# Three passes of rounded parts for the latent tiles of the even stage's output product

## The chip, the cores and the metric

The kernel runs on one core of a Trainium2 chip. A core has TensorE (PE, matrix products into PSUM banks of 128x512 fp32), VectorE (DVE), ScalarE (ACT), GpSimd (POOL) and SyncE (SP), which issues most of the DMAs. The metric is the device time of one execution in microseconds; lower is better.

## The reference

Two blocks of layers work on 256 tokens of 1024 features, in fp32: a windowed attention layer, an expert layer, a recurrent layer and a second expert layer, then an "even" and an "odd" mixing layer. The change lies in the even mixer. It adds the outputs of two attention forms, a gated linear attention (GLA, 4 heads of 128) and a latent attention (MLA, 8 heads of 64), side by side as 1024 features, and multiplies them by one output matrix:

```python
# latent attention of the even mixer, 8 heads, keys = 256 context tokens + 256 tokens
s = (einsum('bqhd,bkhd->bhqk', q_nope, k_nope) + einsum('bqhr,bkr->bhqk', q_rope, k_rope)) * MLA_SCALE
p = softmax(s, axis=-1)
y_m = einsum('bhqk,bkhd->bqhd', p, v).reshape(B, L, 512) * silu(mg)
# y_g: the gated linear attention's output, 512 features
y_lat = einsum('bne,ed->bnd', concatenate([y_g, y_m], -1), w_out)      # 1024 x 1024
x = layer_norm_2(ALPHA * x + gate * y_lat, g, b)
```

## The kernel before

Tokens are held as two halves of 128. Features across partitions are held as tiles of 128: `B.yT` has eight tiles j of 128 features by 256 tokens. Tiles 0 to 3 come from the GLA and 4 to 7 from the latent attention; `GH` is 4 and `T` is 8.

**Two kinds of products.** A product of plain fp32 tiles is one call of `matmul` (L371) and leaves two records in the trace. Where an operand is split into a rounded part (type fp32r, `hi`) and the rest (`lo = x - hi`), `product` (L367 to L374) makes three calls, lo by hi, hi by lo and hi by hi, with one record each. Most weight products of the even and odd stage are of the second kind. `split_weights_scalar` (L396) has ScalarE write the rounded part of a weight unit in four pieces of 128x1024, and `split_weights_vector` (L412) has VectorE write the rest over the raw unit. The even stage's output product is of the first kind, for all its eight tiles.

**The latent rounds.** The even stage interleaves two generators on each engine, a linear one (GLA) and a latent one, one step of each in turn (`even_order`, L2218). After projections come the latent rounds n = 0 to 19 of `latent_tensor`, `latent_vector` and `latent_scalar`; a unit of work i is one head and one half of the tokens, sixteen in all (`NB`). In round n each engine does, in this order:

- TensorE: the scores of n (L2761), four transposes of the probabilities of n-2 (L2773), and in rounds 6, 10, 14 and 18 the value products of latent tile j (L2786) into bank 7. Its linear step follows: GLA's turned output (L2551), then for half 0 and then half 1 one GLA tile of the output product per step, in both column blocks c of 512.
- VectorE: reciprocal and scaling of the probabilities of n-2 (L2843, L2845), then maximum and its negative of the scores of n (L2849, L2851), and in rounds 7, 11, 15 and 19 the gated y of latent tile j (L2861), which writes `B.yT[:, GH + j]`. Its linear steps at this time are the scaled GLA rows (L2638, after rounds 7 and 8) and GLA's gated y (L2648, after rounds 9 and 10).
- ScalarE: exp of the scores of n (L2907), then the copy of the transposed probabilities of n-2 (L2915). After round 14 it rounds pieces 0 and 1 of the odd stage's first weight unit (`odd_sv`), and VectorE subtracts them after round 17.

TensorE's transposes i wait for the event `probs_lat` i, and for the exp of i+1, which frees their bank. The engines work strictly in the order of the program.

**Behind the rounds.** TensorE does the latent tiles of the output product, for half 0 block 0, half 0 block 1, half 1 block 0 and half 1 block 1 (`even_tensor`, L2296 to L2303). After each of these four it tells `out_product`. VectorE then subtracts pieces 2 and 3 of `odd_sv`, and `gated_residual_vector` (L2192) multiplies each block by the gate (L2202), adds it to x (L2204), takes its moments (L514), and norms each half after its second block (L529, L533). The odd stage starts from the normed half 0 on ScalarE (`flat_scalar`, L2172 to L2183), whose rows TensorE transposes (L2088). In between TensorE does two modulation blocks (L964), whose weights SyncE loads into slots that are free after the last latent y.

**Memory.** `even_out0` and `even_out1` are units of the weight ring; each holds its eight tiles as 8 x 512 columns, tiles 4 to 7 in the second half.

Of the kernel before, what the change touches and what calls it, by code (L numbers as in the profile page):

```python
# [9 lines left out]
F32R = mybir.dt.float32r  # L10
ACT = mybir.ActivationFunctionType
ALU = mybir.AluOpType
AX = mybir.AxisListType

P = 128
D = 1024
S = 256
H = S // P
T = D // P
# [4 lines left out]
UNIT = 4096  # L24
# [25 lines left out]
GH, GK, GV, GR, GCH = 4, 64, 128, 16, 64  # L50
# [12 lines left out]
NB = MH * H  # L63
# [283 lines left out]
class Program:  # L347
# [1920 lines left out]
    def even_tensor(self):  # L2268
        sig, pe, B, K = self.sig, self.pe, self.B, self.B.bank
# [26 lines left out]
        _, banks, y, y_event, names, _ = self.even_out()  # L2296
        w = self.out_weights(names)
        for half in range(H):
            for c in range(2):
                for j in range(GH, T):  # L2300
                    pe.wait_ge(*sig.after(*y_event(j)))
                    last = self.out_step(banks[2 * half + c], y, w[c], j, half)
                last.then_inc(*sig.tell("out_product", ("out_product", "even", half, c), ("free", names[c])))  # L2303
# [125 lines left out]


# [360 lines left out]
    def latent_vector(self):  # L2791
        sig, v, B, K = self.sig, self.v, self.B, self.B.bank
# [37 lines left out]
        for j in range(MH // 2):  # L2830
            n = 2 * j
# [7 lines left out]
        for n in range(NB + 4):  # L2839
            if 2 <= n < NB + 2:  # L2840
                i = n - 2
# [15 lines left out]
            if n >= 7 and n % 4 == 3:  # L2857
                j = n // 4 - 1
                v.wait_ge(*sig.after("values_lat", j))
                v.wait_ge(*sig.after("even_taken", "mg0" if j < 2 else "mg2"))  # L2860
                v.tensor_tensor(B.yT[:, GH + j, :], K[7][:, j % 2 * S:(j % 2 + 1) * S], B.mgT[:, j, :], ALU.mult).then_inc(  # L2861
                    *sig.tell("mla_y", ("mla_y", j), ("free", "latents")))
            if n == NB + 1:
                self.split_weights_vector("odd_sv", pieces=(0, 1))
            yield

    def latent_scalar(self):
        sig, a, B, K = self.sig, self.a, self.B, self.B.bank
# [20 lines left out]
        for j in range(MH // 2):  # L2889
            n = 2 * j + 1  # L2890
# [7 lines left out]
        for n in range(NB + 4):  # L2898
# [10 lines left out]
            if 2 <= n < NB + 2:  # L2909
                i = n - 2  # L2910
                h, half = i // H, i % H
# [5 lines left out]
            if n == NB - 2:  # L2917
                self.split_weights_scalar("odd_sv", pieces=(0, 1))
# [325 lines left out]
def buffers(nc, ctx):  # L3244
# [116 lines left out]
    B.yT, B.mgT = M.take("even_yT", T, S), M.take("mgT", GH, S)  # L3361
# [12 lines left out]
    B.att = [M.place(f"att{dd}", h_at + 2048 + 1024 * dd, [4, 2 * P]) for dd in range(2)]  # L3374
    flat_at = M.at
# [11 lines left out]
    B.gla_ss, B.gla_r = M.take("gla_ss", H * GH), M.take("gla_r", H * GH)  # L3387
    M.at = ring + TAIL_SLOT * UNIT
# [62 lines left out]
```

## Time and profile before

| | |
|---|---|
| median of 3 runs | 1420.01 us (1419.85 to 1422.73) |
| profiled execution | 1421.49 us |
| its span | 1419.6 us |
| TensorE busy | 1101.4 us, 78% |
| VectorE busy | 467.2 us, 33% |
| ScalarE busy | 321.2 us, 23% |
| mean granted TensorE clock | 0.893 |

The span is the time from the first to the last instruction of the profiled execution. Most of it, up to about 1140 us, is the experts' weights coming in; the even stage takes the stretch from there to about 1316 us, the odd stage the rest. In rows, "PE" is a matrix product and "PEld" the load of its stationary operand; "xN" is a count of merged instructions, and the time beside it is from the start of the first to the end of the last. A name such as L2845 is a line of the kernel.

### The profile page before, as it was taken

The page shows a single profiled execution, that of the slowest core. Times are in us where ns is not written, and L with a number is a line of the kernel's source. Part 1 is how long each engine was busy: PE and PEld are TensorE (multiplying, and loading weights), DVE is VectorE, ACT ScalarE, POOL GpSimd, SP SyncE. Part 2 cuts the span into 40 slices and gives each one's busy share as a digit, 9 for nine tenths or more (in the row PEclk, how much of TensorE's full clock was granted, in tenths as well). Part 3 has the DMA queues.
Part 4 walks back from the last instruction along what each step waited for, and adds up shares of the span by engine and source line. Part 5 has one row for each costly group of instructions (what it writes and reads, how often), then busy time and mean ns, then how long its engine had stood idle before and what let it go on. Part 6 is the DMA issues. An engine that isn't in the chain of part 4 may idle for free.

```text
span 1419.6 us, 19300 instructions
## 1 busy us (share of the span) xinstructions
PE 1101.4 (78%) x8457; PEld 624.6 (44%) x8457; DVE 467.2 (33%) x952; ACT 321.2 (23%) x618; POOL 86.2 (6%) x114
## 2 busy tenths in 40 slices
PE   8999756598486556999995656766655699999998
PEld 7657312263131112897641211111111279754997
DVE  6636203101110000777630100100000077666774
ACT  4502110000410000465220000000000046543640
POOL 1311100000000000040120000000000000000100
PEclk9999978899688878999997777767898899999999
DMA  9977999999999999958999999999999974113720
GB/s 372 425 292 298 423 427 428 427 428 425 428 427 427 427 427 422 388 201 343 427 383 426 428 427 427 428 427 428 428 427 428 422 308 156 60 74 157 301 95 30
DMA packets 43211, 501.27 MB, mean 353 GB/s; under 512 B 6654, under 2 KB 8148, under 8 KB 13688
## 3 DMA queue, kind: packets, MB, share of 16 engines
q1 hardware_dynamic: 38432, 491.91, 82.9%
q10 hardware_dynamic: 2696, 6.83, 1.3%
q8 instruction: 67, 1.10, 0.3%
q0 software_dynamic: 2000, 1.29, 0.3%
q14 instruction: 16, 0.13, 0.0%
HBM read 498.92 MB, written 1.10 MB: 352 GB/s over the span
## 4 chain that ended last, share of the span: by engine, by line
DMA 45%; PE 42%; DVE 6%; ACT 4%; SPq 1%; issue 1%; POOL 0%; DVEq 0%; ACTq 0%; POOLq 0%
DMA weight_ring<-in_moe_w_gate_up 32%; DMA weight_ring<-in_u_down 8%; PE bank L1437 7%; PE bank L371 5%; PE bank L372 3%; PE bank L374 3%; PE bank L373 3%; PE bank L1467 3%; DMA weight_ring<-in_u_ctx_kv 2%; PE bank L1888 2%; PE bank L653 2%; DMA weight_ring<-in_u_last 2%; DVE weight_ring_rounded L412 2%; SPq L570 1%; PE bank L1079 1%
## 5 line engine op out<-in xcount | busy, mean ns | idle before, releaser
L1437 PE MATMUL bank<-weight_ring,expert_tokens 128*32 128x512 f32 x1920 | 282.3, 722 | 156.5 <-DMA weight_ring<-in_moe_w_gate_up 151.6
L1437 PEld LDWEIGHTS bank<-weight_ring,expert_tokens 128*32 128x32 f32 x1920 | 61.4, 121 | 354.3 <-DMA weight_ring<-in_moe_w_gate_up 197.1
L1467 PE MATMUL bank<-weight_ring,actT 128*32 128x256 f32 x1760 | 141.1, 479 | 56.6 <-DMA weight_ring<-in_u_down 46.9
L1676 DVE TENSOR_TENSOR act<-silu,bank 128x256 f32<-128x256 f32 x32 | 13.5, 420 | 387.2 <-ACT silu L1794 387.2
L1467 PEld LDWEIGHTS bank<-weight_ring,actT 128*32 128x32 f32 x1760 | 65.1, 133 | 122.6 <-issue 48.4
L1794 ACT ACTIVATE silu<-bank 128x256 f32<-128x256 f32 x32 | 12.3, 384 | 436.7 <-PE bank L1437 436.6
L1690 DVE COPY expert_outs<-bank 32x256 f32<-32x256 f32 x60 | 25.1, 418 | 236.0 <-PE bank L1467 235.0
L412 DVE TENSOR_TENSOR weight_ring_rounded<-weight_ring,weight_ring_rounded 128x1024 fp32r<-128x1024 f32 (+1 forms) x76 | 89.3, 1234 | 11.4 <-ACT weight_ring_rounded L396 11.2
L396 ACT CAST weight_ring_rounded<-weight_ring 128x1024 fp32r<-128x1024 f32 (+1 forms) x72 | 69.9, 1045 | 19.1 <-DMA weight_ring<-in_u_even_narrow 8.2
L1811 ACT COPY expert_outs<-bank 32x256 f32<-32x256 f32 x60 | 21.9, 365 | 214.8 <-PE bank L1467 214.0
L539 POOL TENSOR_TENSOR norm_rstd<-norm_var,minus_half 128x1 f32<-128x1 f32 x12 | 11.2, 936 | 838.8 <-DVE norm_var L1725 642.2
L1449 PE MATMUL bank<-ident,act 128*128 128x128 f32 x64 | 17.1, 354 | 41.0 <-DVE act L1676 41.0
L1449 PEld LDWEIGHTS bank<-ident,act 128*128 128x128 f32 x64 | 10.1, 206 | 73.5 <-DVE act L1676 73.5
L417 PE MATMUL bank<-ident 128*128 128x128 f32 x278 | 36.9, 288 | 3.5 <-DMA ident<-in_k_ident 2.6
L417 PEld LDWEIGHTS bank<-ident 128*128 128x128 f32 x278 | 34.5, 201 | 5.7 <-DMA ident<-in_k_ident 2.6
L372 PE MATMUL bank<-odd_h_hi_rounded,weight_ring_rounded 128*128 128x256 f32 x128 | 36.4, 284 | 0.0
L374 PE MATMUL bank<-odd_h_hi_rounded,weight_ring_rounded 128*128 128x256 f32 x128 | 36.2, 283 | 0.0
L373 PE MATMUL bank<-odd_h_rounded,weight_ring_rounded 128*128 128x256 f32 x128 | 36.2, 283 | 0.0
L372 PE MATMUL bank<-even_h_hi_rounded,weight_ring_rounded 128*128 128x256 f32 x96 | 28.6, 298 | 2.5 <-DVE weight_ring_rounded L412 2.4
L371 PE MATMUL bank<-weight_ring,even_yT 128*128 128x512 f32 x64 | 29.3, 597 | 0.0
L371 PE MATMUL bank<-weight_ring,attention_out 128*128 128x512 f32 x64 | 28.1, 594 | 0.0
L1888 PE MATMUL bank<-convolved,weight_ring 128*128 128x256 f32 x128 | 27.8, 379 | 0.0
(528 smaller groups left out, 1848.1 us busy)
## 6 DMA issues: line engine op xcount, KB each, us to landing
weight_ring<-in_moe_w_gate_up SPq DMA_DIRECT2D x120, 2048.0 KB, 36.5
weight_ring<-in_u_down SPq DMA_DIRECT2D x55, 2048.0 KB, 37.1
weight_ring<-in_u_ada SPq DMA_DIRECT2D x8, 2048.0 KB, 11.3
weight_spare<-in_moe_w_gate_up SPq DMA_DIRECT2D x6, 2048.0 KB, 40.7
weight_spare<-in_u_down SPq DMA_DIRECT2D x5, 2048.0 KB, 40.7
weight_ring<-in_u_last SPq DMA_DIRECT2D x16, 512.0 KB, 34.0
weight_ring<-in_u_lru SPq DMA_DIRECT2D x4, 2048.0 KB, 20.8
weight_spare<-in_u_ada SPq DMA_DIRECT2D x3, 2048.0 KB, 13.7
```

Of the source, the lines that this page charges most:

```text
L371: return self.pe.matmul(out, sh, mh, start=start, stop=stop)
L372: self.pe.matmul(out, sl, mh, start=start, stop=False)
L373: self.pe.matmul(out, sh, ml, start=False, stop=False)
L374: return self.pe.matmul(out, sh, mh, start=False, stop=stop)
L396: a.copy(hi[:, c], raw[:, c]).then_inc(*sig.tell("weights_rounded", ("rounded", name, i)))
L412: v.tensor_tensor(lo[:, c], raw[:, c], hi[:, c], ALU.subtract).then_inc(*sig.tell("weights_split", ("weights", name, i)))
L417: self.pe.matmul(bank[:, 0:P], self.B.ident, self.B.ident, start=True, stop=True)
L653: last = pe.matmul(out, *operands, start=(parts == self.HIGH and t == 0 and first), stop=(parts == self.WEIGHTS_REST and t == T - 1), skip ...
L1437: last = pe.matmul(up[CAP * j:CAP * (j + 1), :], self.expert_tokens(t, e), w[:, :, j, :], start=(t == 0), stop=(t == T - 1))
L1449: last = pe.transpose(K[2][:, s * P:(s + 1) * P], B.act[i][:, s::2], B.ident)
L1467: last = pe.matmul(K[3][CAP * q:CAP * (q + 1), 0:QC], B.actT[i][:, s, j * CAP:(j + 1) * CAP], w[:, jj, s, q, :], start=(j == 0 and s == 0) ...
L1888: last = pe.matmul(self.lru_bank(job)[:, ff * S:(ff + 1) * S], w[:, z * LB + n, at:at + P], B.xc[:, 2 * n + c], start=(c == 0), stop=(c == 1))
```

## The change

The four latent tiles of the output product become products of rounded parts. For that:

- in rounds 7, 11, 15 and 19 VectorE forms y twice from PSUM, once as fp32 into `B.yT` and once rounded into `B.y_mla_hi`, and writes their difference over the fp32 one (`B.y_mla_lo`). The event `mla_y` j and the freeing of the latents' memory move to the second of these instructions; a new event `mla_split` j follows the third;
- the second halves of `even_out0` and `even_out1` are split in four pieces of 128x1024: ScalarE rounds piece i in round 8, 10, 12 and 14, after its copy, and waits for the turned GLA output before it; VectorE subtracts it at the end of round 9, 11, 13 and 15. The order is block 0 first piece, block 1 first piece, block 0 second piece, block 1 second piece;
- the latent tiles of each of the four output blocks are three calls per tile, in the order of blocks as before, with waits on `mla_split` and `out_split`;
- ScalarE's rounding of pieces 0 and 1 of `odd_sv` moves from after round 14 to after round 16;
- the new tiles are placed in memory (`mla_y_hi`, `even_out_hi0`, `even_out_hi1`; the differences lie over the raw data).

```diff
--- before.py
+++ after.py
@@ -2293,14 +2293,15 @@
             last.then_inc(*sig.tell("projected", ("even", job), *free))
 
         self.even_order("tensor", run, None, self.linear_tensor(), self.latent_tensor())
-        _, banks, y, y_event, names, _ = self.even_out()
-        w = self.out_weights(names)
-        for half in range(H):
-            for c in range(2):
-                for j in range(GH, T):
-                    pe.wait_ge(*sig.after(*y_event(j)))
-                    last = self.out_step(banks[2 * half + c], y, w[c], j, half)
-                last.then_inc(*sig.tell("out_product", ("out_product", "even", half, c), ("free", names[c])))
+        _, banks, _, _, names, _ = self.even_out()
+        for half, c in ((0, 0), (0, 1), (1, 0), (1, 1)):
+            rows = slice(half * P, (half + 1) * P)
+            for j in range(T - GH):
+                pe.wait_ge(*sig.after("mla_split", j))
+                pe.wait_ge(*sig.after("out_split", c, j // 2))
+                last = self.product(banks[2 * half + c], (B.y_mla_hi[:, j, rows], B.y_mla_lo[:, j, rows]),
+                                    (B.out_hi[c][:, j, :], B.out_lo[c][:, j, :]), start=False, stop=(j == T - GH - 1))
+            last.then_inc(*sig.tell("out_product", ("out_product", "even", half, c), ("free", names[c])))
 
     def even_narrow_tensor(self, w, h):
 
@@ -2427,6 +2428,24 @@
         self.flat_pool("odd", 1)
 
 
+
+    OUT_PIECES = ((0, 0), (1, 0), (0, 1), (1, 1))
+
+    def out_weights_scalar(self, i):
+
+        sig, a, B = self.sig, self.a, self.B
+        c, q = self.OUT_PIECES[i]
+        flat = lambda w: w[c][:, 2 * q:2 * q + 2, :].rearrange("p t c -> p (t c)")
+        a.wait_ge(*sig.after("gla_turned", 1))
+        a.wait_ge(*sig.after("arrived", f"even_out{c}"))
+        a.copy(flat(B.out_hi), flat(B.out_raw)).then_inc(*sig.tell("out_rounded", ("out_rounded", c, q)))
+
+    def out_weights_vector(self, i):
+        sig, v, B = self.sig, self.v, self.B
+        c, q = self.OUT_PIECES[i]
+        flat = lambda w: w[c][:, 2 * q:2 * q + 2, :].rearrange("p t c -> p (t c)")
+        v.wait_ge(*sig.after("out_rounded", c, q))
+        v.tensor_tensor(flat(B.out_lo), flat(B.out_raw), flat(B.out_hi), ALU.subtract).then_inc(*sig.tell("out_split", ("out_split", c, q)))
 
     def odd_or_even(self, buf, kk):
 
@@ -2859,7 +2878,14 @@
                 v.wait_ge(*sig.after("values_lat", j))
                 v.wait_ge(*sig.after("even_taken", "mg0" if j < 2 else "mg2"))
                 v.tensor_tensor(B.yT[:, GH + j, :], K[7][:, j % 2 * S:(j % 2 + 1) * S], B.mgT[:, j, :], ALU.mult).then_inc(
+                    *sig.tell("mla_y", ("mla_y_whole", j)))
+                v.tensor_tensor(B.y_mla_hi[:, j, :], K[7][:, j % 2 * S:(j % 2 + 1) * S], B.mgT[:, j, :], ALU.mult).then_inc(
                     *sig.tell("mla_y", ("mla_y", j), ("free", "latents")))
+                v.wait_ge(*sig.after("mla_y", j))
+                v.tensor_tensor(B.y_mla_lo[:, j, :], B.yT[:, GH + j, :], B.y_mla_hi[:, j, :], ALU.subtract).then_inc(
+                    *sig.tell("mla_split", ("mla_split", j)))
+            if n in (9, 11, 13, 15):
+                self.out_weights_vector(n // 2 - 4)
             if n == NB + 1:
                 self.split_weights_vector("odd_sv", pieces=(0, 1))
             yield
@@ -2914,7 +2940,9 @@
                     a.wait_ge(*sig.after("values_lat", (h - 4) // 2))
                 a.copy(B.pT_lat[h % 4][:, :, half * P:(half + 1) * P], self.latent_bank("t", i).rearrange("p (a b) -> p a b", a=KT)).then_inc(
                     *sig.tell("scalar_moved", ("pT_lat", i)))
-            if n == NB - 2:
+            if n in (8, 10, 12, 14):
+                self.out_weights_scalar(n // 2 - 4)
+            if n == NB:
                 self.split_weights_scalar("odd_sv", pieces=(0, 1))
             yield
 
@@ -3358,7 +3386,8 @@
     B.lru_hi, B.lru_lo = M.take_both("lru_x_hi", T, S)[1], M.take_both("lru_x_lo", T, S)[1]
 
     M.at = room
-    B.yT, B.mgT = M.take("even_yT", T, S), M.take("mgT", GH, S)
+    (B.yT, low), B.mgT = M.take_both("even_yT", T, S), M.take("mgT", GH, S)
+    B.y_mla_lo = low[:, GH:T]
     B.reset, B.tri = M.take("reset", 2, S), M.take("tri", 2, P, dt=U32)
     at = M.at
     B.qT_gla, B.kT_gla = M.take("gla_qT", 2, S), M.take("gla_kT", 2, S)
@@ -3372,6 +3401,7 @@
     B.h_raw["even"], B.h_lo["even"] = M.take_both("even_h", T, S)
     B.state = [[M.place(f"state{dd}{i}", h_at + 256 * (2 * dd + i), [2, GV]) for i in range(2)] for dd in range(2)]
     B.att = [M.place(f"att{dd}", h_at + 2048 + 1024 * dd, [4, 2 * P]) for dd in range(2)]
+    B.y_mla_hi = M.place("mla_y_hi", h_at + 1024, [T - GH, S], F32R)
     flat_at = M.at
     B.flat_stats, B.flat_mv, B.flat_sum = M.take("flat_stats", 12), M.take("flat_mv", 2), M.take("flat_sum", 2)
     B.flat_rstd, B.flat_var, B.flat = M.take("flat_rstd", H), M.take("flat_var", H), M.take("flat", H, D)
@@ -3385,6 +3415,12 @@
     B.ke, B.qe, B.kend, B.qb = ([M.take(f"{n}{dd}", 2, S) for dd in range(2)] for n in ("ke", "qe", "kend", "qb"))
     B.o_gla, B.gla_junk = M.take("gla_out", H, GH * GV), M.place("gla_squares", flat_at, [H, GH * GV])
     B.gla_ss, B.gla_r = M.take("gla_ss", H * GH), M.take("gla_r", H * GH)
+    B.out_hi, B.out_raw, B.out_lo, B.one = [], [], [], M.place("one", M.size - UNIT - 8, [1])
+    for c in range(2):
+        slot = B.place_of[f"even_out{c}"]
+        B.out_hi.append(M.place(f"even_out_hi{c}", M.size - UNIT + c * UNIT // 2, [T - GH, 512], F32R))
+        for dst, ring_view in ((B.out_raw, B.slot), (B.out_lo, B.slot_r)):
+            dst.append(ring_view[slot][:, UNIT // 2:UNIT].rearrange("p (t c) -> p t c", t=T - GH))
     M.at = ring + TAIL_SLOT * UNIT
     B.cq, B.ckr = M.take("cq", H, QR), M.take("ckr", H, CKR)
     B.latT, B.krT = M.take("latT", KEYS), M.take("krT", KEYS)[0:MR, :]
```

## Rows read from the trace of the kernel before

**Rows 1.** Windows: us, busy PE, PEld, DVE, ACT, POOL, then clock, DMA share, GB/s
```profile
1262.00:1272.00 10.00, 7.33 (x43) 4.37 (x44) 8.32 (x23) 4.89 (x12) 1.00 (x1) 1.00 0.00 1
1272.00:1298.00 26.00, 26.00 (x111) 12.94 (x107) 10.74 (x27) 11.36 (x22) 0.00 (x0) 1.00 0.05 20
```

**Rows 2.** Chain of what ended last, even stage's end: start, us, what
```profile
1269.57 0.50 DVE mla_scores L2845
...
1298.01 7.08 PE bank L371 x16
...
1315.87 0.70 PE bank L2088 x4
```

**Rows 3.** Time line of TensorE: start, us, line, out<-in, [idle before <-releaser]
```profile
1264.95 0.63 PE L2773 MATMUL bank<-ident,mla_scores 128*128 128x128 f32 x4 [1.30 <-DVE mla_scores L2845]
...
1270.20 0.63 PE L2773 MATMUL bank<-ident,mla_scores 128*128 128x128 f32 x4 [1.14 <-DVE mla_scores L2845]
...
1278.33 0.60 PE L2773 MATMUL bank<-ident,mla_scores 128*128 128x128 f32 x4
...
1284.37 0.60 PE L2773 MATMUL bank<-ident,mla_scores 128*128 128x128 f32 x4
...
1291.63 0.63 PE L2773 MATMUL bank<-ident,mla_scores 128*128 128x128 f32 x4
...
1297.94 14.00 PE L371 MATMUL bank<-weight_ring,even_yT 128*128 128x512 f32 x32
```

**Rows 4.** Time line of VectorE, latent rounds, residual, and one later weight group
```profile
1276.31 0.41 DVE L2861 TENSOR_TENSOR even_yT<-bank,mgT 128x256 f32<-128x256 f32 x1
1276.64 0.15 DVE L2843 RECIPROCAL mla_tot<-mla_tot 128x1 f32<-128x1 f32 x1
1276.83 0.49 DVE L2845 TENSOR_SCALAR mla_scores<-mla_scores,mla_tot 128x512 f32<-128x512 f32 x1
...
1282.54 0.49 DVE L2845 TENSOR_SCALAR mla_scores<-mla_scores,mla_tot 128x512 f32<-128x512 f32 x1
...
1291.00 0.49 DVE L2845 TENSOR_SCALAR mla_scores<-mla_scores,mla_tot 128x512 f32<-128x512 f32 x1
...
1298.06 0.42 DVE L2861 TENSOR_TENSOR even_yT<-bank,mgT 128x256 f32<-128x256 f32 x1 [3.71 <-PE bank L2786]
1298.40 2.35 DVE L412 TENSOR_TENSOR weight_ring_rounded<-weight_ring,weight_ring_rounded 128x1024 fp32r<-128x1024 f32 x2
...
1305.11 0.69 DVE L2202 TENSOR_TENSOR even_tmp<-bank,gate 128x512 f32<-128x512 f32 x1 [1.22 <-PE bank L371]
...
1326.71 4.63 DVE L412 TENSOR_TENSOR weight_ring_rounded<-weight_ring,weight_ring_rounded 128x1024 fp32r<-128x1024 f32 x4 [0.24 <-ACT weight_ring_rounded L396]
```

**Rows 5.** Time line of TensorE, first and eighth record of the odd output product
```profile
1390.64 0.40 PE L372 MATMUL bank<-weight_ring_rounded,odd_yT_rounded 128*128 128x512 f32 x1
...
1392.25 0.39 PE L373 MATMUL bank<-weight_ring_rounded,odd_y_hi 128*128 128x512 f32 x1
```

**Rows 6.** Tile view of the modulation weights' loads (in_u_ada), issued at 1298.5 and 1298.9
```profile
DMA to landing us min/median/max: 7.5/10.4/13.3
```

**Rows 7.** Time line of ScalarE in the latent rounds
```profile
1266.30 0.58 ACT L2915 COPY mla_pT<-bank 128x512 f32<-128x512 f32 x1
...
1268.71 0.69 ACT L2907 ACTIVATE mla_scores<-bank,mla_neg 128x512 f32<-128x512 f32 x1 [1.83 <-DVE mla_neg L2851]
...
1286.63 2.00 ACT L396 CAST weight_ring_rounded<-weight_ring 128x1024 fp32r<-128x1024 f32 x2
...
1294.45 0.59 ACT L2915 COPY mla_pT<-bank 128x512 f32<-128x512 f32 x1 [1.57 <-PE bank L2773]
```

**Rows 8.** Waits from 1262 to 1298: who for whom, us in total, times, longest
```profile
DVE mla_neg L2849 <- PE bank L2761: 12.8, 7, 3.6
```

**Rows 9.** Window and TensorE's time line at the start of the even stage
```profile
1154.00:1162.00 8.00, 5.77 (x32) 5.32 (x30) 4.37 (x9) 6.58 (x14) 0.55 (x1) 0.79 1.00 428
...
1156.61 1.91 PE L2088 MATMUL bank<-ident,flat 128*128 128x128 f32 x8 [2.23 <-ACT flat L2164]
```

## The prediction

> **What bounds the kernel now.** I read the views from the coarse to the fine. First the windows of the latent rounds: TensorE is busy 26.00 of 26 us between 1272 and 1298, and 7.33 of 10 us between 1262 and 1272, where VectorE is busy 8.32 us [rows 1]. So there are two regimes: one stretch in which VectorE sets the pace, then one in which TensorE does. Then the chain of what ended last: at 1298.01 it runs through sixteen records of the output product, then through VectorE's residual and norm and ScalarE's flat rows, and at 1315.87 back to TensorE [rows 2]. Hence two questions. What does the added VectorE work do to the rounds, and how much of the shorter product reaches VectorE's residual?
>
> The third view is the time line of TensorE [rows 3]. I call the transposes of round i's probabilities t(i); they have L2773, and each stands behind VectorE's scaling of the probabilities at L2845, p(i). t(6) at 1264.95 and t(8) at 1270.20 wait for p (1.30 and 1.14 us idle). t(10), t(12) and t(14), at 1278.33, 1284.37 and 1291.63, show no idle time, but that alone says nothing on how much slack they have. For that the fourth view, VectorE's time line [rows 4]: p(10) begins at 1276.83 and takes 0.49, p(12) begins at 1282.54, p(14) at 1291.00. From the end of p(8), 1269.57 + 0.50 in the chain [rows 2], to t(8) there are about 0.15 us, so TensorE could have gone on at 1277.47, 1283.18 and 1291.64. The slack is 0.86 for t(10), 1.19 for t(12) and nothing for t(14): TensorE and VectorE arrive there together, though no view reports a wait.
>
> **The change, part by part.**
>
> *a. Three passes for four latent tiles.* Sixteen fp32 products (4 tiles, 2 halves, 2 column blocks), 32 records in 14.00 us from 1297.94, so a pace of 14.00 / 32 = 0.4375 with the overhang of the last record, 0.43 without, and 0.86 a product [rows 3]. The new products have 3 records of 128x512 of rounded parts. Their pace is that of the odd stage's output product: seven paces from 1390.64 to 1392.25, 0.230 each [rows 5]. The stationary part is reloaded before each there too, as it will be here. 48 records are 11.0 us instead of 13.8, and TensorE is done 2.8 us sooner. The path asks for another thing, the end of half 0, block 1, which is what VectorE waits for at 1305.11 [rows 4]. Before it lie 16 records, 6.88 us; then 24, 5.52 us: 1.36 sooner, at 1303.75. Is VectorE free for it by then? The first block comes after 12 x 0.23 = 2.8 us instead of 3.4, but VectorE has the steps of c and two weight pieces ahead of it, to 1298.06 + 1.13 + 2.35 = 1301.5. The first block's three steps, each of about 0.7 like that at 1305.11, end at 1303.6. So the second block's end rules, and this part is **minus 1.3** (minus 1.36, less what little VectorE may be late).
> What is late next: the modulation blocks at L964 follow the products. The second block of their weights lands 13.3 us after its issue, the largest of the two [rows 6], so near 1312.2, and the issue waits for the last y (about 0.4 us later now). 64 of 128 small products after that, 1.8 us, end at 1314.5; the half-0 transposes come at 1315.87 - 1.3 = 1314.6. Just covered; at worst 0.1 us. All of the odd stage's path behind it moves as one.
>
> *b. Weight pieces.* ScalarE rounds four pieces of 128x1024 and VectorE subtracts, in rounds 8, 10, 12, 14 and 9, 11, 13, 15. The weights themselves landed long before (output products use them from 1272 on without waiting). Price on VectorE: two such pieces take 2.35 us and four 4.63, so 1.14 each [rows 4]. Price on ScalarE: 1.0, two having taken 2.00; its copy of round 8 runs from 1266.30 to 1266.88, and the next exp is at 1268.71 [rows 7]. The new cast waits for the second group of turned gla tiles, which TensorE finishes where that copy ends; it fits before the exp. Behind the waiting cast are queued that exp and, on VectorE, the piece of round 9. So **ScalarE's part costs nothing**, with some 0.5 us of room in round 8 and more later; without that cover up to 1.0 us. Queued behind a VectorE piece are p(i) and, behind that, TensorE's t(i).
>
> *c. Rounded y.* The product y is formed twice from PSUM, then a subtraction waits for both. y to the next start is 0.33 [rows 4]; the second y adds 0.33, ends 0.42 after its start, the subtraction starts 0.04 later and holds the next for 0.34 (same 256 columns). From the first y's start to the next instruction: 0.33 + 0.42 + 0.04 + 0.34 = 1.13 instead of 0.34, **0.79 more** each, in rounds 7, 11, 15, 19. Bounds: 0.67 if the subtraction needs no wait, 0.9 if all three run their full 0.42 with a wait behind each. The row is exact for the product and near for the subtraction, so the middle.
> The Trainium skill, page "VectorE: DVE Perf Modes", section "The DRAIN you can't avoid", has the next instruction start only when the pipe is empty, and a semaphore costing nothing extra. The rows have y to the next start at 0.33 and its length at 0.42 [rows 4], so this trace doesn't agree for instructions that don't depend on one another. By the page c would be 0.93 and a piece 1.22, and the sum some 0.6 us more.
>
> *d. Where b and c meet the rounds.*
> Round 7: 0.79 lies before the scaled gla rows (L2638) and p(6), and t(6) already waits: **+0.79**. Everything up to t(8) moves along: VectorE's one gap in between waits for scores that TensorE, itself held by the gla rows, delivers later too.
> Round 9: 1.14 before gla's y and p(8), t(8) already waits: **+1.14**.
> Round 11: c and b, 1.93, before p(10), slack 0.86: **+1.07**.
> Round 13: b, 1.14, before p(12), slack 1.19: **0** (at most 0.1).
> Round 15: c and b, 1.93, before p(14), slack 0: **+1.93**.
> Between these, TensorE has 26.00 of 26 us and nothing is given back [rows 1]. Sum **+4.9**.
> Round 19: y(3) at 1298.06, its parts done 1.2 us later; tile 3 of the first block is reached 9 x 0.23 = 2.07 us after 1297.94. Hidden by 0.7 us.
>
> *e. Moved pieces of the odd weights.* ScalarE's two casts go from after round 14 to after round 16's copy: about 1292.9 to 1294.9, then the last copy of probabilities, old start 1294.45 [rows 7], comes some 0.4 late and ends at 1295.4, before the value products, which end at 1297.94. VectorE's two subtractions then end near 1296.2, before y(3) at 1298.06. Zero; if the cover went, 0.4.
>
> **Sum**: 0.79 + 1.14 + 1.07 + 1.93 - 1.3 = +3.6 us. The profiled execution is 1421.49 us with a span of 1419.6, and its sum is 1425.1. The median of the runs shown is 1420.01, 1.5 us below it; the same 3.6 on the median gives **1423.6**.
>
> **Rivals.**
> R1, cover: VectorE waits 12.8 us in all for TensorE's scores from 1262 to 1298 [rows 8], and the 6.9 us added there (3 x 0.79 + 4 x 1.14) would fit into that if they fell into the right places. Then the tail's -1.3 alone is left: 1418.7, not slower. Against it: both t(6) and t(8) wait on VectorE by name, and p(14) leaves no slack; idle time ahead of the scores is of no use to a step that stands behind them. It decides if p could be formed ahead of the new pieces, which the order in the file forbids.
> R2, half cover: only the two places where TensorE waits today grow (1.93), and rounds 11 and 15 hide theirs: 1.93 - 1.3 = +0.6, 1420.6. For it: no view shows a wait there. Against it: the worked slack.
> R3, the clock: TensorE stood still for 2.23 us before 1156.61, and over the 8 us from 1154 its granted clock averages 0.79, so it was at 1.2 GHz for part of them [rows 9]. The pauses at t(6), t(8) and t(14) grow to 2.09, 2.28 and 1.93. If one of them drops the clock, it costs what that stretch lost, 0.21 x 8 = 1.7 us: 1425.3; two, 1427. Against it: the pauses of 1.30 and 1.14 left it at 1.00 [rows 1]. [...]
> R4, no cheaper passes: were each of the three as long as a third of an fp32 product (0.285), a would bring nothing and the sum is +4.9, 1424.9. The odd stage's records speak against it.
>
> **Chances.** Forecast (+2.9 to +4.5) 0.56; R3 0.07; another added delay 0.05; R4 0.02; R2 and its neighbours 0.14; R1 0.12; something that I don't see and that gains 0.04. By these the low end is taken to 1420.2, so that R2 is in and R1 out, the high end to 1427.0 for R3; the unknown costs (0.36 for c, 0.6 for the drain, 0.4 for e) lie within. A measurement of this kernel can tell about 0.2%, 2.8 us, from no change. R1 and R2 lie within it. Even with every edit hidden, the path gains no more than 1.4 us, so faster by over 0.2% takes something that no row shows. From the forecast's 0.56 some 0.03 go to no change: slower 0.53 + 0.07 + 0.05 + 0.02, rounded to 0.66, same 0.14 + 0.12 + 0.03 = 0.29, faster 0.05.
>
> **What would show it.** In the changed profile: gaps before t(6) and t(8) of about 2.1 and 2.3 us, new ones before t(10) of 1.1 and t(14) of 1.9, all named to p; none before t(12); the last latent product block of 48 records in about 11 us; its start 4.9 us later than 1297.94; first residual of half 0 to second with no gap; granted clock 1.00 in the rounds. Wrong would make me: no gap before t(14), a cast on ScalarE that holds an exp, or a gap before tile 3 of the first block.

## The result and the profile after

The changed kernel takes 1425.25 us (median; 1422.46 to 1426.18), the kernel before 1420.93 us (1419.42 to 1423.03) beside it. The ratio is 1.0029, 95% interval 1.0021 to 1.0037, so +4.1 us with bounds of +3.0 and +5.3. The forecast was +3.6.

In the profiles the latent rounds do not begin at the same moment each time: over all runs the scores of round 8 start up to 2.2 us sooner or 0.9 us later than before. The variation lies ahead of them, in the start of the even stage (its first transposes start between 1155.79 and 1157.94) and in the granted clock behind it (0.79 or 1.00 from 1154 to 1162, 0.96 or 1.00 from 1200 to 1240), where all these kernels do the same. To take it out, every position below is counted from the scores of round 8 on TensorE, 1262.62 before and 1262.63 in the changed kernel, and "against before" means after that correction. The medians contain that scatter, so a part of a microsecond is read from positions.

A figure in us beside a ratio is that ratio taken on the median of the kernel before. The ratio comes from all runs, so it isn't exactly that of the two medians.

TensorE's time line of the changed kernel; columns as in [rows 3], L2780 are the scores, L2792 the transposes t(i), L2570 the turned gla rows (L2773 before is now L2792, and so on). p(i) is VectorE's scaling of round i's probabilities, now L2864. It stands beside [rows 3].

```profile
1262.63 1.02 PE L2780 MATMUL bank<-mla_kT,mla_qT 96*128 96x512 f32 x2
1265.76 0.94 PE L2792 MATMUL bank<-ident,mla_scores 128*128 128x128 f32 x4 [2.10 <-DVE mla_scores L2864]
1266.49 1.91 PE L2570 MATMUL bank<-ident,gla_out 128*128 128x128 f32 x8
1268.20 1.59 PE L2780 MATMUL bank<-mla_kT,mla_qT 96*128 96x512 f32 x2
...
1273.36 0.63 PE L2792 MATMUL bank<-ident,mla_scores 128*128 128x128 f32 x4 [2.27 <-DVE mla_scores L2864]
...
1282.56 0.63 PE L2792 MATMUL bank<-ident,mla_scores 128*128 128x128 f32 x4 [0.90 <-DVE mla_scores L2864]
...
1288.62 0.60 PE L2792 MATMUL bank<-ident,mla_scores 128*128 128x128 f32 x4
...
1297.80 0.63 PE L2792 MATMUL bank<-ident,mla_scores 128*128 128x128 f32 x4 [1.77 <-DVE mla_tot L2862]
...
1304.11 0.50 PE L372 MATMUL bank<-even_out_hi,even_yT_rounded 128*128 128x512 f32 x1
```

The pauses before t(6), t(8), t(10) and t(14) are all there, 2.10, 2.27, 0.90 and 1.77 us, and none before t(12). (A row counts its pause from the end of the record ahead, which overlaps the next one by about 0.16 us where TensorE doesn't wait, so the new pauses of 0.90 and 1.77 are delays of 1.07 and 1.92.) (The note names the reciprocal L2862 of the next round for t(14), since that ended last by the record; it starts after p(14).) Taking [rows 3] away: t(6) is 0.8 us later than before, t(8) 3.2, t(10) 4.2, t(12) 4.2, t(14) 6.2, and so are the latent products, 1304.11 after 1297.94. The steps from one to the next are those of the working, except between t(6) and t(8): 2.35 us instead of 1.14. There the same instructions are longer. For the kernel before, TensorE's time line in that place:

```profile
1266.24 0.66 PE L2551 MATMUL bank<-ident,gla_out 128*128 128x128 f32 x4 [0.23 <-DVE gla_out L2638]
1266.74 1.02 PE L2761 MATMUL bank<-mla_kT,mla_qT 96*128 96x512 f32 x2
```

Four transposes of gla rows took 0.66 us, now eight take 1.91, and the two score records 1.59 instead of 1.02. The windows of the changed kernel say why; columns are those of [rows 1]:

```profile
1264.00:1266.00 2.00, 0.24 (x2) 0.27 (x3) 1.97 (x5) 0.57 (x2) 0.00 (x0) 0.98 0.00 0
1266.00:1268.00 2.00, 2.00 (x12) 2.00 (x11) 1.52 (x5) 1.25 (x3) 0.00 (x0) 0.50 0.00 0
1268.00:1270.00 2.00, 2.00 (x8) 1.13 (x7) 0.17 (x1) 1.04 (x1) 0.00 (x0) 0.66 0.00 0
```

The granted clock is 0.50, that is 1.2 GHz, from 1266 to 1268 and 0.66 in the mean, partly back at 2.4 GHz, in the next 2 us. Ahead of it TensorE was busy 0.24 of 2 us. In the kernel before it is 1.00 over 1262 to 1272 [rows 1].

VectorE's time line, changed kernel, beside [rows 4]: the three instructions of y in round 7, a weight piece in round 9, then the tail.

```profile
1263.20 0.42 DVE L2880 TENSOR_TENSOR even_yT<-bank,mgT 128x256 f32<-128x256 f32 x1
1263.54 0.41 DVE L2882 TENSOR_TENSOR mla_y_hi<-bank,mgT 128x256 fp32r<-128x256 f32 x1
1263.99 0.42 DVE L2885 TENSOR_TENSOR even_yT_rounded<-even_yT,mla_y_hi 128x256 fp32r<-128x256 f32 x1
1264.34 0.68 DVE L2657 TENSOR_TENSOR gla_out<-bank,gla_r 128x512 f32<-128x512 f32 x1
...
1270.62 1.21 DVE L2448 TENSOR_TENSOR weight_ring_rounded<-weight_ring,even_out_hi 128x1024 fp32r<-128x1024 f32 x1
1271.76 0.87 DVE L2667 SCALAR_TENSOR_TENSOR even_yT<-bank,parameter_columns,ggT 128x256 f32<-128x256 f32 x2
...
1307.63 0.69 DVE L2202 TENSOR_TENSOR even_tmp<-bank,gate 128x512 f32<-128x512 f32 x1
...
1309.99 0.69 DVE L2202 TENSOR_TENSOR even_tmp<-bank,gate 128x512 f32<-128x512 f32 x1 [0.21 <-PE bank L374]
```

y to the next instruction is 1.14 instead of 0.34, and the piece holds the next for 1.14. At the end the first block's residual (1307.63) waits for nothing on TensorE, and the second (1309.99) starts after a wait of 0.21 us for TensorE: 4.88 us later than before, while the products began 6.17 us later. The tail gives back 1.29.

### The profile page after: what moved, and what is told of

Same layout as the page of the kernel before. It is cut to its first block, busy times and chain, and to the rows that moved or that the text cites. A ratio compares the mean times of both kernels' runs of the same rounds, so it can differ in the third digit from the quotient of the medians.

```text
span 1424.5 us, 19350 instructions
## 1 busy us (share of the span) xinstructions
PE 1099.8 (77%) x8473; PEld 630.6 (44%) x8473; DVE 474.3 (33%) x964; ACT 324.8 (23%) x622; POOL 86.0 (6%) x114
## 3 DMA queue, kind: packets, MB, share of 16 engines
q0 software_dynamic: 2000, 1.29, 0.3%
## 4 chain that ended last, share of the span: by engine, by line
DMA 46%; PE 42%; DVE 6%; ACT 3%; SPq 1%; issue 1%; POOL 0%; DVEq 0%; ACTq 0%; POOLq 0%
DMA weight_ring<-in_moe_w_gate_up 32%; DMA weight_ring<-in_u_down 8%; PE bank L1437 7%; PE bank L371 5%; PE bank L372 3%; PE bank L374 3%; PE bank L373 3%; PE bank L1467 3%; DMA weight_ring<-in_u_ctx_kv 2%; PE bank L1888 2%; PE bank L653 2%; DMA weight_ring<-in_u_last 2%; DVE weight_ring_rounded L412 1%; SPq L570 1%; PE bank L964 1%
## 5 line engine op out<-in xcount | busy, mean ns | idle before, releaser
L372 PE MATMUL bank<-even_h_hi_rounded,weight_ring_rounded 128*128 128x256 f32 x96 | 28.6, 297 | 2.4 <-DVE weight_ring_rounded L412 2.4
L1484 PE MATMUL bank<-expert_outs,back 128*128 128x512 f32 x48 | 25.1, 657 | 4.9 <-DVE expert_outs L1690 4.0
L374 PE MATMUL bank<-even_h_hi_rounded,weight_ring_rounded 128*128 128x256 f32 x96 | 27.8, 290 | 0.0
```

The costliest lines, as they stand in the source:

```text
L372: self.pe.matmul(out, sl, mh, start=start, stop=False)
L374: return self.pe.matmul(out, sh, mh, start=False, stop=stop)
```

## The experiments

Two theories stand against each other. **Place**: what the change adds on VectorE costs only where it stands ahead of something TensorE waits for, with the sizes of the prediction's steps, and the pauses that this lengthens let the clock fall, which costs again. **Amount**: VectorE simply has more work in the stage, and the cost follows the amount. All runs are set against the kernel before, in medians and in positions. The cuts of code leave out what doesn't matter for the argument; words in brackets stand for code.

### The tail alone

```diff
-    v.tensor_tensor(B.yT[:, GH + j, :], K[7][...], B.mgT[:, j, :], ALU.mult)      # whole
-    v.tensor_tensor(B.y_mla_hi[:, j, :], K[7][...], B.mgT[:, j, :], ALU.mult)     # rounded
-    v.tensor_tensor(B.y_mla_lo[:, j, :], B.yT[...], B.y_mla_hi[...], ALU.subtract)
+    v.tensor_tensor(B.y_mla_lo[:, j, :], K[7][...], B.mgT[:, j, :], ALU.mult)     # serves as both parts
-    if n in (9, 11, 13, 15):
-        self.out_weights_vector(n // 2 - 4)                                       # out_hi serves as both parts
```

> Leaves out VectorE's rounded y, its rest and the four subtractions of the weights: the products take three records each, but of tiles that are not split, so only their time is the changed kernel's. Theory (the cost sits in the rounds, where added VectorE steps stand ahead of the scaling that TensorE waits for): rounds as before, start of the latent products within 0.1 us of 1297.94, VectorE's second residual 1.3 us sooner than 1305.11, total -1.3 us against the kernel before. Rival (the three-pass products themselves cost what was lost): the total stays above the kernel before, by 3 us or more.

Measured: ratio 0.9988 (0.9979 to 0.9998), -1.7 us. Positions of this run on TensorE (scores 8, t(14)) and VectorE (second residual):

```profile
1262.80 1.02 PE L2780 MATMUL bank<-mla_kT,mla_qT 96*128 96x512 f32 x2
...
1291.81 0.63 PE L2792 MATMUL bank<-ident,mla_scores 128*128 128x128 f32 x4
```

```profile
1304.03 0.69 DVE L2202 TENSOR_TENSOR even_tmp<-bank,gate 128x512 f32<-128x512 f32 x1 [0.58 <-PE bank L374]
```

t(14) lies 29.01 us behind the scores of round 8, as before. The second residual is at 1304.03 - 0.18 = 1303.85 instead of 1305.11, 1.26 sooner. So the three-pass products bring 1.3 us, ScalarE's casts and the moved casts cost nothing, and all the loss in the rounds comes with VectorE's added instructions.

### One part of VectorE's work each

`no_y_split` has the first half of the diff above, `no_w_pieces` the second.

> Leaves out the second y and its rest (y is written once, rounded, and serves as both parts); the four weight pieces stay. Theory: round 7 costs 0, round 9 1.14, round 11 1.14 - 0.86 = 0.28, round 15 1.14, sum 2.6, with the tail -1.3: +1.3 us against the kernel before; the pause before t(6) is 1.3 us again and TensorE's clock stays at 1.00 around 1266 to 1270. Rival (cost in proportion to the added VectorE work, wherever it stands): 4.6 of 7.7 us are left, so 0.59 x 6.2 - 1.3 = +2.3 us.

> Leaves out VectorE's four subtractions of the weights (the rounded weights serve as both parts); ScalarE's casts and the split y stay. Theory: round 7 costs 0.79 and makes the pause before t(6) 2.1 us, after which the clock falls for some 3 us as in the changed kernel and costs 1.2 more; rounds 9 and 11 cost 0 (0.79 is under the slack of 0.86), round 15 0.79. Sum 1.6 + 1.2 - 1.3 = +1.5 us against the kernel before, +0.3 in an execution in which the clock doesn't fall. Rival (in proportion): 3.2 of 7.7 us are left, +1.2 us, and gaps before t(10) as well.

Measured: without the split y 1.0015 (1.0006 to 1.0024), +2.1 us; without the weight pieces 1.0004 (0.9995 to 1.0013), +0.6 us, which a measurement can't tell from nothing. TensorE without the split y, and a window of it:

```profile
1261.43 1.02 PE L2780 MATMUL bank<-mla_kT,mla_qT 96*128 96x512 f32 x2
...
1270.14 0.63 PE L2792 MATMUL bank<-ident,mla_scores 128*128 128x128 f32 x4 [2.27 <-DVE mla_scores L2864]
1270.70 3.31 PE L2805 MATMUL bank<-mla_pT,mla_values 128*64 128x256 f32 x16
...
1294.64 0.63 PE L2792 MATMUL bank<-ident,mla_scores 128*128 128x128 f32 x4 [0.98 <-DVE mla_tot L2862]
```

```profile
1272.00:1274.00 2.00, 2.00 (x11) 0.80 (x7) 0.16 (x1) 1.02 (x2) 0.00 (x0) 0.50 0.66 248
```

The pause before t(6) is 1.30 as before the change, that before t(8) 2.27, and t(10) has about the 0.28 expected. The clock does fall here, though, behind t(8): sixteen value records take 3.31 us, not 1.95, at 0.50 around 1273. I expected it at 1.00 and so was short: t(14) is 4.20 us later against before, 2.6 by the working and 1.6 by the clock. TensorE without the weight pieces:

```profile
1261.81 1.02 PE L2780 MATMUL bank<-mla_kT,mla_qT 96*128 96x512 f32 x2
1264.93 1.09 PE L2792 MATMUL bank<-ident,mla_scores 128*128 128x128 f32 x4 [2.10 <-DVE mla_scores L2864]
...
1293.60 0.63 PE L2792 MATMUL bank<-ident,mla_scores 128*128 128x128 f32 x4 [0.65 <-DVE mla_tot L2862]
```

The pause before t(6) is 2.10 and those further on are as in the kernel before up to t(14), whose position is 2.78 us later against before: 0.79 + 0.79 and 1.2 for a fall of the clock behind t(6), as expected. At t(10) 0.79 is under the slack of 0.86 and adds nothing. Its median is nearer to the expectation without a fall. The amount theory isn't yet excluded by the medians: it had +2.3 and +1.2, and +2.1 and +0.6 were measured.

### The same work in another order

```diff
+    if n in (8, 12, 17) or n == NB + 3:       # behind p(n-2), ahead of the maximum of n
+        (y whole, y rounded, rest of y for tile 0, 1, 2, 3)
+    if n in (10, 12, 14, 17):
+        self.out_weights_vector(...)
     if n < NB:
         v.tensor_reduce(B.lat_neg[:, n:n + 1], self.latent_bank("s", n), AX.X, ALU.max)
-    if n >= 7 and n % 4 == 3:
-        (y whole, y rounded, rest of y)
-    if n in (9, 11, 13, 15):
-        self.out_weights_vector(n // 2 - 4)
```

> The changed kernel's whole VectorE work in another order: each y with its two parts, and each weight piece, stands behind the scaling p of the following round instead of ahead of it. Theory (only what stands ahead of an awaited p or of the gla rows costs): round 7's 0.79 stays by way of the second gla rows, rounds 9, 11 and 15 cost 0; no pause over 1.5 us, so no fall of the clock; 0.8 - 1.3 = -0.5 us against the kernel before. Rival (cost in proportion to the added VectorE work): the same work costs the same, +4.3.

Measured: 0.9991 (0.9982 to 1.0000), -1.3 us. The same instructions in the same number, and 5 us less than in the changed kernel. This excludes the amount theory. TensorE:

```profile
1260.46 1.02 PE L2780 MATMUL bank<-mla_kT,mla_qT 96*128 96x512 f32 x2
...
1264.86 0.66 PE L2570 MATMUL bank<-ident,gla_out 128*128 128x128 f32 x4 [1.35 <-DVE gla_out L2657]
...
1290.23 0.60 PE L2792 MATMUL bank<-ident,mla_scores 128*128 128x128 f32 x4
```

The 0.79 of round 7 comes by the second group of gla rows (1.35 us idle instead of 0.23). t(14) is 0.76 us later against before, as expected, and the clock stays at 1.00. The tail returns less than 1.3 here, 1.0 by the position of the odd stage's first transposes, since the second modulation block waits 1.78 us for its weights and they follow it directly. That is the cover of step a, used up. By position the whole gain is then 0.3 us at these transposes, less than the 1.3 of the medians, though inside their interval.

### The clock

Two kernels put dummy products into the pauses, and a third run repeats the changed kernel. The first fills the pause before t(6) alone:

```diff
+    if i == 6:
+        (waits for bank 0 to be free)
+        self.idle_products_tensor(K[0], 6)        # six products nobody reads
     pe.wait_ge(*sig.after("probs_lat", i))
```

> The changed kernel with six small dummy products of TensorE (1.4 us) put into the pause of 2.1 us before t(6). Theory (the longer pause lets the granted clock fall, and that costs 1.24 us between t(6) and t(8)): granted clock 1.00 from 1264 to 1270, t(7) 0.8 us later than before instead of 2.0, rounds +4.9 instead of +6.2, total 1.2 us under the changed kernel, +3.6 against the kernel before. Rival (the slow transposes after t(6) have another cause, such as banks shared with VectorE): no change, +4.9.

Measured: 1.0030 (1.0019 to 1.0042), +4.3 us, not +3.6. TensorE around t(8) and the window behind it:

```profile
1273.06 0.63 PE L2796 MATMUL bank<-ident,mla_scores 128*128 128x128 f32 x4 [2.27 <-DVE mla_scores L2868]
1273.62 3.56 PE L2809 MATMUL bank<-mla_pT,mla_values 128*64 128x256 f32 x16
```

```profile
1274.00:1276.00 2.00, 2.00 (x12) 1.19 (x10) 1.04 (x4) 1.94 (x4) 0.00 (x0) 0.50 0.54 201
```

Behind t(6) the clock is now 1.00, and it falls behind t(8) instead, after the pause of 2.27 us that in the changed kernel had left it alone. The value products take 3.56 us. So the dummies removed one fall and another took its place, a dearer one: t(14) is 6.58 us later against before, and the expected 1.2 us less did not come. The next run fills all three pauses:

```diff
     self.latent_free("t", i)
+    if i in (6, 8, 14):
+        (waits for bank 7 to be free)
+        self.idle_products_tensor(K[7][:, S:2 * S], {6: 6, 8: 7, 14: 6}[i])
     pe.wait_ge(*sig.after("probs_lat", i))
```

> The changed kernel with small dummy products of TensorE in all three long pauses, before t(6), t(8) and t(14), since with only the first filled the clock fell after the second instead (value products behind t(8) 3.56 us instead of 1.95). Theory (the falls of the clock are the 1.2 us by which the rounds cost more than the working without them): granted clock 1.00 through all latent rounds, rounds +4.9 us and the total +3.6 against the kernel before. Rival (dummies shift the cost but some other slowness remains, or they delay the transposes themselves): +4.3 or more.

Measured: 1.0021 (1.0012 to 1.0030), +3.0 us. The window of the rounds, and TensorE:

```profile
1260.00:1300.00 40.00, 37.49 (x178) 20.96 (x174) 26.57 (x63) 19.26 (x37) 1.64 (x1) 1.00 0.05 17
```

```profile
1295.63 0.66 PE L2797 MATMUL bank<-ident,mla_scores 128*128 128x128 f32 x4 [0.35 <-DVE mla_scores L2869]
```

The clock is 1.00 throughout, t(14) is 4.79 us later against before (the scores of round 8 start at 1261.83), and the span of 1422.4 us is 3.6 longer once the earlier start (0.79) is taken out. This is the prediction's sum with its clock. Last, the changed kernel once more, without any edit, for a second profile:

> The changed kernel once more, for a second profile. Theory: the positions of VectorE's and TensorE's instructions repeat within 0.1 us apart from the clock, and the clock falls again after one of the two pauses over 2 us, behind t(6) or behind t(8); total +4.3 against the kernel before, against +2.8 for the run with all pauses filled. Rival (the fall was an accident of one execution): clock 1.00 in the latent rounds and +3.0.

Measured: 1.0041 (1.0027 to 1.0055), +5.8 us from five runs; the two medians are 4.9 apart. The scores of round 8 start at 1262.02.

```profile
1265.14 0.63 PE L2792 MATMUL bank<-ident,mla_scores 128*128 128x128 f32 x4 [2.10 <-DVE mla_scores L2864]
...
1266.93 1.90 PE L2780 MATMUL bank<-mla_kT,mla_qT 96*128 96x512 f32 x2
...
1272.40 0.63 PE L2792 MATMUL bank<-ident,mla_scores 128*128 128x128 f32 x4 [1.47 <-DVE mla_scores L2864]
```

```profile
1266.00:1270.00 4.00, 3.77 (x13) 2.24 (x12) 2.04 (x6) 2.33 (x5) 0.00 (x0) 0.62 0.00 0
```

The pause before t(6) is 2.10 again and the clock falls again, a little later: the gla rows are still at full speed, the scores of round 9 take 1.90. t(8) is 2.80 us later against before, of which 1.93 is VectorE's and 0.87 the clock's (3.15 - 1.93 = 1.22 in the first profile). So it repeats, with a varying size. That it falls in every execution isn't shown, two profiles being all there is.

The start of the even stage bears this out in all eleven profiles. TensorE waits there for ScalarE's flat rows, a place that the change doesn't touch, and the pause differs from one execution to the next. After 2.23, 2.27, 2.28, 2.32 and 2.45 us the granted clock from 1154 to 1162 is 0.79, as in [rows 9]; after 1.28, 1.40, 1.48, 1.64, 1.73 and 1.78 us it is 1.00. The longest pause without a fall, in `filled_pause`:

```profile
1157.94 1.13 PE L2088 MATMUL bank<-ident,flat 128*128 128x128 f32 x8 [1.78 <-ACT flat L2164]
```

```profile
1154.00:1162.00 8.00, 5.16 (x41) 4.79 (x40) 5.12 (x9) 7.01 (x14) 0.55 (x1) 1.00 1.01 432
```

So in this kernel the pauses that cost the clock are those above 2 us, in two places. What decides between two such pauses, when only one brings a fall, isn't shown.

### Versions without the cost

`into_gaps` has all of the change's work, put where the engines wait anyway, with ScalarE making the rounded part of y for three tiles. ScalarE's casts of the weights also move, to rounds 9, 10, 12 and 13, and those of `odd_sv` back to round 14:

```diff
+    for i in {11: (0, 1), 15: (2, 3)}.get(n, ()):      # VectorE, behind p(9) and p(13)
+        self.out_weights_vector(i)
+    if n in (11, 13, 17):                              # rests of y, tiles 0, 1, 2
+        self.latent_rest_vector(...)
+    if n in (10, 11, 16):                              # ScalarE rounds y, tiles 0, 1, 2
+        a.copy(B.y_mla_hi[:, j, :], B.yT[:, GH + j, :])
```

> All of the change's work, put where VectorE waits for scores: the weight pieces two and two behind p(9) and p(13), the rests of y in rounds 11, 13 and 17, and ScalarE instead of VectorE rounds y for the first three tiles. Theory: the rounds cost nothing, t(14) within 0.1 us of the kernel before, and the tail's gain alone is left, -1.3 us. Rival (some of the added work has a cost of its own, such as ScalarE's casts holding an exp): over -0.5 us.

Measured: 1419.14 us beside 1420.67, ratio 0.9990 (0.9981 to 0.9999), -1.4 us.

```profile
1291.12 0.63 PE L2799 MATMUL bank<-ident,mla_scores 128*128 128x128 f32 x4
```

```profile
1303.30 0.69 DVE L2202 TENSOR_TENSOR even_tmp<-bank,gate 128x512 f32<-128x512 f32 x1
```

t(14) lies 29.01 us behind the scores of round 8 (1262.11): the rounds cost nothing. The second residual is 1.30 sooner against before. `tiles_early` builds on it:

```diff
-    for half in range(H):                                  # TensorE, one step per latent round
-        for j in range(GH): gla tile j of half
+    gla tiles 0 to 3 of half 0; latent tile 0 of half 0; gla tile 0 of half 1; latent tiles 1, 2 of half 0
+    tail: gla tile 1 of half 1, latent tile 3 of half 0, gla tiles 2, 3 of half 1, latent tiles of half 1
```

> The kernel of the run into_gaps with another order of TensorE's products: the first three latent tiles of half 0 stand in rounds 14, 16 and 17 in place of gla tiles of half 1, which follow in the tail; of half 0 only tile 3 is left behind the last y. One modulation block comes behind the transposes of the odd stage's half 0 in place of dummy products, and one piece of the odd weights behind half 0's residual. Theory (the path runs through half 0's second block, then VectorE's norm and ScalarE's flat rows): that block is ready 3.2 us sooner than in the kernel before, total -3.0 us. Rival (half 1 then becomes the path, or the modulation weights' landing does): -1.3 us as in into_gaps.

Measured: 1416.44 us beside 1420.67, ratio 0.9979 (0.9970 to 0.9988), -3.0 us, the fastest of all (the two medians are 4.2 apart). VectorE's second residual, and TensorE's transposes of the odd stage for half 0 and half 1:

```profile
1310.43 1.14 PE L2088 MATMUL bank<-ident,flat 128*128 128x128 f32 x8 [1.13 <-ACT flat L2183]
...
1316.97 1.13 PE L2088 MATMUL bank<-ident,flat 128*128 128x128 f32 x8 [0.24 <-DVE flat L2153]
```

```profile
1299.91 0.68 DVE L2202 TENSOR_TENSOR even_tmp<-bank,gate 128x512 f32<-128x512 f32 x1
```

With the scores of round 8 at 1260.73, the residual is 3.3 us (1299.91 + 1.89 against 1305.11) and half 0's transposes are 3.6 us (1310.43 + 1.89 against 1315.87) sooner. The theory's path doesn't hold to the end, though. Half 1's transposes wait for VectorE, and the chain of what ended last runs back from them through half 1's norm and residual, the moved weight piece (1.13 us) and half 0's norm, nearly all of it on VectorE. They are 3.2 us sooner (1316.97 + 1.89 against 1322.02), and 3.0 is left at the end. So half 1 did become the path, as the rival had it, but at -3.0 and not at -1.3.

### All runs side by side

The aligned span is the profile's span against before, with the start of round 8 taken out; t(14) likewise. In all but `tiles_early`, the stretch from half 0's transposes of the odd stage to the end is 103.7 to 103.9 us long (104.3 there), so the scatter lies ahead.

| run | us by the ratio (its interval) | aligned span, us | t(14), us |
|---|---|---|---|
| changed kernel | +4.1 (+3.0 to +5.3) | +4.9 | +6.2 |
| the same again | +5.8 (+3.8 to +7.8) | +4.6 | +5.8 |
| `tail_alone` | -1.7 (-3.0 to -0.3) | -1.2 | 0.0 |
| `no_y_split` | +2.1 (+0.9 to +3.4) | +3.0 | +4.2 |
| `no_w_pieces` | +0.6 (-0.7 to +1.8) | +1.6 | +2.8 |
| `scaling_first` | -1.3 (-2.6 to 0.0) | -0.1 | +0.8 |
| `filled_pause` | +4.3 (+2.7 to +6.0) | +5.5 | +6.6 |
| `filled_all` | +3.0 (+1.7 to +4.3) | +3.6 | +4.8 |
| `into_gaps` | -1.4 (-2.7 to -0.1) | -1.2 | 0.0 |
| `tiles_early` | -3.0 (-4.3 to -1.7) | -3.0 | -0.3 |

Each aligned span lies inside the interval beside it, and most lie above the ratio's figure, by up to 1.2 us; why isn't known.

## Why the prediction was right, step by step

- **a, the products.** Gain on the path 1.3 forecast, 1.29 in the changed kernel, 1.26 with the tail alone. The 48 records go from 1304.11 to the modulation block at 1315.45, 11.3 us, where 11.0 was worked out. VectorE free before the second block: yes, by 0.21 us (the sign "first residual of half 0 to second with no gap" didn't fit the prediction's own times of 1303.6 and 1303.75). The landing of the modulation weights, "just covered": the second block waited 1.36 us for it, but ScalarE's flat rows end at 1320.59 and the transposes follow them at 1320.74, at the distance of before (0.15) and 4.87 us later, like the residual. The landing became visible in `scaling_first`.

```profile
1315.45 1.93 PE L964 MATMUL bank<-weight_ring,condition_columns 128*2 128x128 f32 x64
1318.74 1.93 PE L964 MATMUL bank<-weight_ring,condition_columns 128*2 128x128 f32 x64 [1.36 <-DMA weight_ring<-in_u_ada]
1320.74 1.13 PE L2088 MATMUL bank<-ident,flat 128*128 128x128 f32 x8
```

- **b, the weight pieces.** 1.14 on VectorE, as measured. ScalarE's room in round 8 held. With the clock at 1.00 (`filled_all`) it is as forecast: the cast follows the copy, and the exp still waits 0.73 us for VectorE after it:

```profile
1266.93 1.05 ACT L2441 CAST even_out_hi<-weight_ring 128x1024 fp32r<-128x1024 f32 x1
1268.71 0.69 ACT L2938 ACTIVATE mla_scores<-bank,mla_neg 128x512 f32<-128x512 f32 x1 [0.73 <-DVE mla_neg L2875]
```

  In the first profile of the changed kernel the cast waits for the turned gla rows, which the clock had slowed:

```profile
1268.44 1.04 ACT L2441 CAST even_out_hi<-weight_ring 128x1024 fp32r<-128x1024 f32 x1 [0.75 <-PE bank L2570]
```

  The exp came later too, by the same cause.
- **c, the split y.** 0.79 forecast, 0.80 measured. The instructions that don't wait for one another start before the one ahead has ended (0.34 for a length of 0.42), as in [rows 4]. The Trainium skill, page "VectorE: DVE Perf Modes", section "The DRAIN you can't avoid", adds to its rule that an instruction which isn't held starts earlier; these runs agree with that clause, which the prediction's reading left out. With the full lengths the sum would have been 0.6 us more, and the run with the clock at 1.00 has 4.79 at t(14), not 5.5.
- **d, the places.** 0.79, 1.14, 1.07, 0 and 1.93 forecast; 0.8, 1.13, 1.07, 0.0 and 1.92 measured, the second as the rise in the pause before t(8), the others as steps between transposes. The slack worked out for t(14), nothing where no view showed a wait, was the term that mattered most, and it was right. Sum 4.93 forecast, 4.92 by these steps, 4.79 in `filled_all` with the clock at 1.00, where t(6) starts 0.1 us sooner behind the dummies than behind a pause.
- **e, the moved casts.** Nothing, as forecast: with the tail alone they are moved too, and t(15) and the values come where they did.
- **What was missed** is the clock. R3 stood at a chance of 0.07, with the argument that pauses of 1.30 and 1.14 had left it at 1.00. The forecast "granted clock 1.00 in the rounds" was wrong: it fell in both profiles of the changed kernel, for 1.22 and 0.87 us, where R3 had 1.7. In aligned spans it is the step from +3.6 (all filled) to +4.9 and +4.6. The ratios show less, their intervals overlapping, but the windows show the fall itself. What happened is thus the forecast's steps with R3's fall added, at a smaller price.
- **Luck** has a part in how near the figure is. The forecast's steps without the clock make +3.6; with it the profile has +4.9, and the medians' +4.1 is lower than that by an amount that no run explains. In absolute time, 1425.25 is 1.65 us above the 1423.6 forecast, of which 0.9 is the kernel before itself, at 1420.93 in these runs and 1420.01 in those that the prediction started from. The end of the range at 1427.0 had been set by R3.
- **R1 and R2** fell by the pauses, and R1 by `scaling_first` and `into_gaps` in a useful way: VectorE's idle time does hold all the work, if it is placed there. R4 fell by the pace of the records, 0.23 us.

## What to carry to other kernels

A step added on an engine costs that part of its length that exceeds the slack of the step behind it: here nothing in round 13, 1.07 of 1.93 us in round 11, all of it in round 15. Idle time ahead of the added step doesn't help. So work out when the awaited result is ready and when its reader arrives, also where no view shows a wait, and put added work directly behind the awaited result rather than ahead of it. Lengthened pauses of TensorE are to be priced twice, once as a pause and once as a possible fall of its clock.

## What the runs showed of the chip

- After a pause of 2.10 us TensorE was granted 1.2 GHz in both profiles of the changed kernel and in `no_w_pieces`, and after one of 2.27 us in two variants (3.31 and 3.56 us for sixteen value records of 1.95). It did not fall after that same 2.27 us in the changed kernel, where it had fallen already at the pause before, nor after pauses of 1.77, 1.47, 1.30 or 1.14. At the start of the even stage it fell after all five pauses of 2.23 to 2.45 us and after none of the six of 1.28 to 1.78. One fall in the rounds cost 0.9 to 1.7 us. The Trainium skill, page "TensorE: Matmul & The Clock Gate", section "Why this matters for your kernels", warns only of idle gaps between bursts that are longer than all of these pauses. This trace doesn't agree, and the measurement decides. Dummy products in one pause moved the fall to the next; in all pauses they kept the clock up, and gained 1.0 to 1.3 us of aligned span although TensorE did more work.
- An output product of 512 columns of plain fp32 (two records) took 0.86 us, the three records of rounded parts 0.70 us (0.23 each). The stationary part is loaded anew before each record.
- On VectorE an instruction that doesn't wait for the one ahead starts before that has ended: 0.34 us after its start for a length of 0.42 (128x256), 1.14 for 1.21 (128x1024). One that waits for it starts 0.03 to 0.04 us after its end.
